# Attention scores with 128-row operands: queries' high and low parts stacked, keys doubled across the rows

## What is computed

```python
def rms_norm(x, g): return x * rsqrt(mean(x * x) + 1e-6) * g     # per head of 64
u = h @ w_qkv                                   # 16 query heads, 4 key heads, 4 value heads
q, k, v = split(u); q = rms_norm(q, qn_g); k = rms_norm(k, kn_g)
s = einsum('bnqkgd,bnskd->bkgnqs', q, k) / 8    # a chunk of 64 frames sees itself and the two before
s = s - slope[head] * |qpos - kpos|;  s = where(valid, s, -1e30)
p = exp(s - m) / (sum(exp(s - m)) + exp(sink - m));  o = p @ v;  x = x + o @ w_o
x = x + (silu(h @ w_gate) * (h @ w_up)) @ w_down                # h = rms_norm of x, d_ff 2816
```

## Time and profile before

| | |
|---|---|
| median of 3 runs | 2325.01 us (2325.01 to 2325.84) |
| the profiled execution's own time | 2324.02 us |
| its span in the trace | 2322.2 us |
| mean granted TensorE clock | 0.989 of full |
| busy: TensorE, VectorE, ScalarE, GpSimd | 2263.4, 1096.5, 1024.8, 1114.9 us |
| half A's attention (scores to values) | about 842 to 1224 us |
| half B's attention | about 1444 to 1824 us |

### The profile page before, as it was taken

How to read it: one execution, slowest core, us unless ns; L and a number is a source line. 1 busy time by engine, 2 the same in 40 slices (tenths; PEclk the granted TensorE clock), 3 DMA queues, 4 the chain that set the end, 5 groups by cost and what they waited for, 6 DMA issues and landing times.

```text
span 2322.2 us, 34761 instructions
## 1 busy us (share of the span) xinstructions
PE 2263.4 (97%) x14082; PEld 2034.6 (88%) x14082; DVE 1096.5 (47%) x1802; ACT 1024.8 (44%) x1639; POOL 1114.9 (48%) x573
## 2 busy tenths in 40 slices
PE   8998899999999999999999999999999999999999
PEld 7897678887888799999999898888888889999999
DVE  4986768863434434444443543444544242232223
ACT  6544655533425545445442465454554332222222
POOL 3787669975455433323333643333333444434442
PEclk9999899999999999999999999999999999999999
DMA  4111223332333322222222333222222223332322
GB/s 147 47 55 55 64 65 103 97 95 89 93 100 87 81 75 76 70 73 64 75 72 84 91 77 84 81 80 75 73 82 73 84 81 96 96 103 89 91 82 94
DMA packets 311437, 191.55 MB, mean 82 GB/s; under 512 B 40214, under 2 KB 285550, under 8 KB 311278
## 3 DMA queue, kind: packets, MB, share of 16 engines
q1 hardware_dynamic: 309400, 188.21, 27.2%
q10 hardware_dynamic: 1878, 1.11, 0.2%
HBM read 184.39 MB, written 5.10 MB: 82 GB/s over the span
## 4 chain that ended last, share of the span: by engine, by line
PE 91%; POOL 3%; DVE 2%; ACT 2%; issue 1%; DMA 0%; ACTq 0%; DVEq 0%; POOLq 0%
PE ps L337 41%; PE ps L346 21%; PE ps L553 14%; PE ps L560 7%; PE ps L523 2%; POOL accp L1920 2%; PE ps L483 1%; PE ps L509 1%; PE ps L355 1%; PE ps L484 1%; PE ps L485 1%; POOL wlo L1889 1%; PE ps L372 1%; DVE x L1573 1%; DVE sq L1382 1%
## 5 line engine op out<-in xcount | busy, mean ns | idle before, releaser
L1889 POOL TENSOR_TENSOR wlo<-raw,whi 128x1024 fp32r<-128x1024 f32 x342 | 839.7, 2455 | 1131.6 <-PE ps L346 802.9
L840 ACT ACTIVATE whi<-raw 128x1024 fp32r<-128x1024 f32 x342 | 361.6, 1057 | 638.7 <-PE ps L337 379.7
L337 PE MATMUL ps<-hBh,whi 128*128 128x272 f32 x2112 | 440.2, 289 | 8.2 <-DVE x L1573 3.3
L337 PE MATMUL ps<-hBl,whi 128*128 128x272 f32 x2112 | 439.4, 289 | 0.0
L337 PE MATMUL ps<-hAh,whi 128*128 128x512 f32 x1056 | 417.9, 396 | 18.5 <-DVE hAl L1387 10.9
L337 PE MATMUL ps<-hAl,whi 128*128 128x512 f32 x1056 | 415.4, 393 | 0.0
L1573 DVE TENSOR_TENSOR x<-ps,x 128x512 f32<-128x512 f32 (+1 forms) x368 | 258.3, 705 | 243.9 <-PE ps L560 181.4
L337 PEld LDWEIGHTS ps<-hBh,whi 128*128 128x128 f32 x2112 | 332.9, 189 | 11.4 <-issue 5.0
L337 PEld LDWEIGHTS ps<-hBl,whi 128*128 128x128 f32 x2112 | 331.6, 189 | 0.0
L346 PE MATMUL ps<-hBh,wlo 128*128 128x272 f32 x2112 | 293.7, 291 | 0.0
L346 PEld LDWEIGHTS ps<-hBh,wlo 128*128 128x128 f32 x2112 | 273.0, 188 | 6.3 <-issue 1.9
(11 more groups left out here) (249 smaller groups left out, 3196.3 us busy)
## 6 DMA issues: line engine op xcount, KB each, us to landing
raw<-in_w_gate_dram SPq DMA_DIRECT2D x88, 512.0 KB, 3.8
raw<-in_w_up_dram SPq DMA_DIRECT2D x88, 512.0 KB, 3.8
raw<-in_w_down_dram SPq DMA_DIRECT2D x88, 512.0 KB, 3.5
raw<-in_w_pw_dram SPq DMA_DIRECT2D x38, 512.0 KB, 3.9
raw<-in_w_qkv_dram SPq DMA_DIRECT2D x32, 256.0 KB, 3.7
raw<-in_w_o_dram SPq DMA_DIRECT2D x64, 128.0 KB, 2.9
stage<-in_x_prompt_dram SPq DMA_DIRECT2D x8, 512.0 KB, 5.4
raw<-in_w_qkv_dram SPq DMA_DIRECT2D x8, 512.0 KB, 3.9
```

What stands on the lines that cost most here:

```text
L337: ins = nc.tensor.matmul(o, whi[n % 2][:, P * k:P * (k + 1)], src[:, k, c0:c0 + w], start=(k == 0 and src is hi_[h]), stop=False)
L840: nc.scalar.activation(whi[n % 2][:], raw[n % 2][:], ACT.Copy).then_inc(w_hi, 1)
L1889: nc.gpsimd.tensor_tensor(wlo[n % 2][:], raw[n % 2][:], f(whi[n % 2][:]), ALU.subtract).then_inc(w_lo, 1)
```

## The change

The parts of a query head are stacked on all 128 partitions. For an even key group `hi_[h]` holds the head's high part on partitions 0-63 and its low part on 64-127; for an odd group `lo_[h]` holds the low part below and the high part above. `kkh` and `kkl` get one plane for each of the four key groups, with the same keys on both halves of the partitions. One matmul of 128 rows then gives high by `kkh` plus low by `kkh`, a second one the same with `kkl`: two matmuls a head for three. (The product low by low comes in with the second.)

- `q_high` and `q_low` become two instructions each, on 64 partitions and 512 columns; the samples' parts keep their own `qsh` and `qsl`, and the samples' scores stay as they were, with keys in `skh` and `skl`.
- `key_high` and `key_low` write each group's half of the partitions in two instructions. SP copies each half to the other half by four DMAs inside SBUF of 256 KB, issued ahead of the load of query tile 4's weights and behind a wait for `kv_lo`. In half A two more DMAs, ahead of query tile 6's, copy the last block of 128 keys to the front, where half B's first tile looks for it. Half B's keys overwrite half A's.
- TensorE waits for `k_twice` ahead of a half's first scores.
- The order of units goes from g0, g0, g1, g1, ... to g0, g1, g0, g1, g2, ..., because two groups now share a tile of `hi_` and `lo_` until both have been scored.
- Small arrays share space (`ssink` and `small` lie in `col`, `ckv` where `dwc` and `stc` were, the four `sco` are one array).

```diff
@@ -174,14 +180,12 @@
...
         with ExitStack() as c:
-            kkh = sb("kkh", [P, 2, TP + WIN + TS], F32R, c)
-            kkl = sb("kkl", [P, 2, TP + WIN + TS], F32R, c)
+            kkh = sb("kkh", [P, 4, 5 * P], F32R, c)
+            kkl = sb("kkl", [P, 4, 5 * P], F32R, c)
+            skh = sb("skh", [P, 2, WIN + TS], F32R, c)
+            skl = sb("skl", [P, 2, WIN + TS], F32R, c)
             vth = sb("vth", [P, 7, 2 * P], F32R, c)
             vtl = sb("vtl", [P, 7, 2 * P], F32R, c)
-            with ExitStack() as c2:
-                ckv = sb("ckv", [P, 2, 2 * P], F32, c2)
-            qsh = sb("qsh", [P, 2, 4 * TS], F32R, c)
-            qsl = sb("qsl", [P, 2, 4 * TS], F32R, c)
         with ExitStack() as c:
...
@@ -261,15 +266,19 @@
...
             u = 4 * beta + b + (32 if h == "B" else 0)
-            g, ip = beta // 2, beta % 2
+            g, ip = 2 * (beta // 4) + beta % 2, beta // 2 % 2
             t = b + (4 if h == "B" else 0)
...
             if t == 0:
-                return u, g, ip, b, 0, P, [(P, slot(0))]
-            return u, g, ip, b, P * (t - 1), 2 * P, [(P, slot(t - 1)), (P, slot(t))]
+                return u, g, ip, b, P, P, [(P, slot(0))]
+            return u, g, ip, b, P * b, 2 * P, [(P, slot(t - 1)), (P, slot(t))]
...
@@ -469,27 +478,25 @@
...
                     pe.wait_ge(kv_lo, 2 if h == "A" else 5)
+                    pe.wait_ge(k_twice, 16 * (4 if h == "A" else 10))
                     for key in [("vt", h, 0), ("vt", h, 1)] + ([("ck",), ("vs",)] if h == "B" else []):
...
                 if beta < 8:
-                    r = slice(HD * (g % 2), HD * (g % 2 + 1))
                     for s in range(2):
...
                         o = ps[:, 4, nk * s:nk * (s + 1)]
-                        qh, ql = (z[h][r, i, P * tl:P * (tl + 1)] for z in (hi_, lo_))
-                        kh, kl = (z[r, g // 2, k0:k0 + nk] for z in (kkh, kkl))
-                        nc.tensor.matmul(o, qh, kh, start=True, stop=False)
-                        nc.tensor.matmul(o, qh, kl, start=False, stop=False)
-                        ins = nc.tensor.matmul(o, ql, kh, start=False, stop=True)
+                        q = (hi_, lo_)[g % 2][h][:, i, P * tl:P * (tl + 1)]
+                        nc.tensor.matmul(o, q, kkh[:, g, k0:k0 + nk], start=True, stop=False)
+                        ins = nc.tensor.matmul(o, q, kkl[:, g, k0:k0 + nk], start=False, stop=True)
                 else:
...
                         qh, ql = qsh[r, b, :], qsl[r, b, :]
-                        kh, kl = (z[r, b, TP:TP + nk] for z in (kkh, kkl))
+                        kh, kl = (z[r, b, :] for z in (skh, skl))
                         nc.tensor.matmul(o, qh, kh, start=True, stop=False)
...
@@ -794,12 +801,22 @@
...
-            def qkv():
+            def qkv(h):
                 for gp in range(2):
...
                 for i in range(KD):
+                    if i == 4:
+                        sp.wait_ge(kv_lo, 2 if h == "A" else 5)
+                        for z in (kkh, kkl):
+                            for e in range(2):
+                                sp.dma_start(f(z[HD * (1 - e):HD * (2 - e), e:4:2, P:5 * P]),
+                                             f(z[HD * e:HD * (e + 1), e:4:2, P:5 * P])).then_inc(k_twice, 16)
+                    if i == 6 and h == "A":
+                        sp.wait_ge(k_twice, 16 * 4)
+                        for z in (kkh, kkl):
+                            sp.dma_start(f(z[:, :, 0:P]), f(z[:, :, 4 * P:5 * P])).then_inc(k_twice, 16)
                     n = slot(("q", i))
...
@@ -1103,7 +1120,8 @@
...
                     nc.scalar.activation(qsh[:, i // 4, TS * (i % 4):TS * (i % 4 + 1)], qraw[i][:, 512:512 + TS], ACT.Copy)
-                nc.scalar.activation(hi_[h][:, i, :], qraw[i][:, dest(h)], ACT.Copy).then_inc(h_hi[h], 1)
+                nc.scalar.activation(hi_[h][0:HD, i, 0:512], qraw[i][0:HD, 0:512], ACT.Copy)
+                nc.scalar.activation(lo_[h][HD:P, i, 0:512], qraw[i][HD:P, 0:512], ACT.Copy).then_inc(h_hi[h], 1)
...
@@ -1135,11 +1153,12 @@
...
                 src = qraw[7 - gp]
-                if h == "A":
-                    nc.scalar.activation(kkh[:, gp, 0:512], src[:, 0:512], ACT.Copy).then_inc(kv_hi, 1)
-                else:
-                    nc.scalar.activation(kkh[:, gp, 512:TP], src[:, 0:512], ACT.Copy)
-                    nc.scalar.activation(kkh[:, gp, TP + WIN:], src[:, 512:512 + TS], ACT.Copy).then_inc(kv_hi, 1)
+                if h == "B":
+                    nc.scalar.activation(skh[:, gp, WIN:], src[:, 512:512 + TS], ACT.Copy)
+                for e in range(2):
+                    r = slice(HD * e, HD * (e + 1))
+                    ins = nc.scalar.activation(kkh[r, 2 * gp + e, P:5 * P], src[r, 0:512], ACT.Copy)
+                ins.then_inc(kv_hi, 1)
...
@@ -1681,19 +1700,20 @@
...
                     nc.vector.tensor_tensor(qsl[z], qraw[i][:, 512:512 + TS], f(qsh[z]), ALU.subtract)
-                nc.vector.tensor_tensor(lo_[h][:, i, :], qraw[i][:, dest(h)], f(hi_[h][:, i, :]), ALU.subtract
+                e, o, n = slice(0, HD), slice(HD, P), slice(0, 512)
+                nc.vector.tensor_tensor(hi_[h][o, i, n], qraw[i][e, n], f(hi_[h][e, i, n]), ALU.subtract)
+                nc.vector.tensor_tensor(lo_[h][e, i, n], qraw[i][o, n], f(lo_[h][o, i, n]), ALU.subtract
                                         ).then_inc(h_ready[h], 1)
...
                 src = qraw[7 - gp]
-                if h == "A":
-                    nc.vector.tensor_tensor(kkl[:, gp, 0:512], src[:, 0:512], f(kkh[:, gp, 0:512]), ALU.subtract
-                                            ).then_inc(kv_lo, 1)
-                else:
-                    nc.vector.tensor_tensor(kkl[:, gp, 512:TP], src[:, 0:512], f(kkh[:, gp, 512:TP]), ALU.subtract)
-                    nc.vector.tensor_tensor(kkl[:, gp, TP + WIN:], src[:, 512:512 + TS], f(kkh[:, gp, TP + WIN:]),
-                                            ALU.subtract).then_inc(kv_lo, 1)
+                if h == "B":
+                    nc.vector.tensor_tensor(skl[:, gp, WIN:], src[:, 512:512 + TS], f(skh[:, gp, WIN:]), ALU.subtract)
+                for e in range(2):
+                    z = (slice(HD * e, HD * (e + 1)), 2 * gp + e, slice(P, 5 * P))
+                    ins = nc.vector.tensor_tensor(kkl[z], src[z[0], 0:512], f(kkh[z]), ALU.subtract)
+                ins.then_inc(kv_lo, 1)
...
```

More of the change, by code:

```diff
@@ L127, in build @@
         ones_h = sb("ones_h", [P, P])
-        col = sb("col", [P, NCOL])
-        dwc = sb("dwc", [P, TAPS * KD])
-        stc = sb("stc", [P, PAD * KD])
+        col = sb("col", [P, NCOL + 41])
+        with ExitStack() as c:
+            dwc = sb("dwc", [P, TAPS * KD], F32, c)
+            stc = sb("stc", [P, PAD * KD], F32, c)
+        with ExitStack() as c:
+            ckv = sb("ckv", [P, 2, 2 * P], F32, c)
+        qsh = sb("qsh", [P, 2, 4 * TS], F32R)
+        qsl = sb("qsl", [P, 2, 4 * TS], F32R)
         nsink = sb("nsink", [P, NH])
-        ssink = sb("ssink", [P, 4])
-        small = sb("small", [P, 37])
+        ssink = col[:, NCOL:NCOL + 4]
+        small = col[:, NCOL + 4:]
         eps, gqn, mn, den = small[:, 0:2], small[:, 2:3], small[:, 3:11], small[:, 11:19]
@@ L166, in build @@
             vo = sb("vo", [P, 2, 2 * P], F32, c)
-        sco = [sb(f"sco{s}", [P, 2, 2 * P + 1]) for s in range(4)]
+        sco = sb("sco", [P, 4, 2, 2 * P + 1])
+        sco = [sco[:, s] for s in range(4)]
         pth = sb("pth", [P, 4 * P], F32R)
@@ L216, in build @@
         hsq, hrs, qn_ready, kv_hi, kv_lo = sem("hsq"), sem("hrs"), sem("qn_ready"), sem("kv_hi"), sem("kv_lo")
+        k_twice = sem("k_twice")
         ko_ready, vo_ready = sem("ko_ready"), sem("vo_ready")
@@ L812, in _ @@
                 load(("p2", d), W2[:, :, P * d:P * (d + 1)])
-            qkv()
+            qkv("A")
             ffn(0, "B")
             wo()
-            qkv()
+            qkv("B")
             ffn(1, "A")
@@ L1168, in qkv_slot @@
                         full(act, ("ck",))
-                        nc.scalar.activation(kkh[:, :, TP:TP + WIN],
+                        nc.scalar.activation(skh[:, :, 0:WIN],
                                              ps[:, place["ck",][0], 0:256].rearrange("p (g n) -> p g n", g=2),
@@ L1720, in qkv @@
                             dve.wait_ge(kv_hi, 6)
-                            nc.vector.tensor_tensor(kkl[:, :, TP:TP + WIN],
+                            nc.vector.tensor_tensor(skl[:, :, 0:WIN],
                                                     ps[:, place["ck",][0], 0:256].rearrange("p (g n) -> p g n", g=2),
-                                                    f(kkh[:, :, TP:TP + WIN]), ALU.subtract).then_inc(fr(("ck",)), 1)
+                                                    f(skh[:, :, 0:WIN]), ALU.subtract).then_inc(fr(("ck",)), 1)
                             dve.wait_ge(kv_hi, 7)
```

## The result

| | before | after |
|---|---|---|
| median of 4 runs each | 2325.32 us (2325.01 to 2325.84) | 2288.37 us (2286.99 to 2289.63) |
| profiled execution, its span | 2324.02, 2322.2 | 2286.99, 2285.2 |
| busy: VectorE, ScalarE, GpSimd | 1096.5, 1024.8, 1114.9 | 1111.8, 1037.8, 1113.6 |

The change makes the kernel faster: the ratio of times is 0.9843, with an interval of 0.9831 to 0.9855. Forecast were 2284.8 us and a range of 2279 to 2298.

The account below looks back on a forecast made before the run. TensorE was taken as the bound. Fewer matmuls (15.0 us) and removed row switches (25) sum to 40.2 us, all else nothing: 2324.0 - 40.2 = 2283.8, as a median 2284.8 us, range 2279.0 to 2298.0.

Parts of the forecast that it names:

- The bound: Whole kernel: TensorE bounds it, busy 97% of the span and 91% of the chain that ended last.
- The switch: Score groups: going to 64-row operands and back costs TensorE 0.39 us a group; removing it saves 25 us.
- The count: Attention scores: 128 fewer matmuls at 0.118 or 0.11 us each save 15.0 us.
- The split instructions: Query and key parts on ScalarE and VectorE: each split costs a second full instruction, hidden behind TensorE, so nothing.
- The stretch by GpSimd: VectorE's two-input instructions stretch beside GpSimd's weight remainder, 2.85 us for 0.7; the split puts more there, costing nothing.
- The queue: SP's copies inside SBUF ahead of query weight loads: taken as costing nothing, 1.1 us late at most.
- the 3.6 of the bound: SP queue: upper limit of 3.6 us per 256 KB copy one after the other, 14.4 us for four.
- Any score group: Rival: the 0.39 us belongs to every score group, not 64 rows; only the matmul saving remains, 2310.0; chance 0.05.
- only the entering half: Rival: the step on entering score groups stays, 64 x 0.19 = 12.2 us come back, 2297.0; chance 0.08.
- spacing doubled: Rival: 128-row score matmuls are spaced at 0.23 us, so about 10 us of saving remain, 2315; chance 0.01.
- the copies: Rival: copies hold up SP's weight loads; at 10 us a copy 53 us are lost, 2338; chance 0.03.
- The stalls at VectorE: Rival: TensorE's 1.3 us waits for VectorE in the steps down multiply, 20 us come back, 2304; chance 0.04.

Follow-up runs that it names:

- the alternating run: Changed kernel with each head's first matmul reading only 64 rows and the second all 128; 2335.84 us.
- after_act_only: Changed kernel with 64 bytes saved ahead of the activation buffers: these at their old address, turned probabilities still 32 bytes off a multiple of 64; 2289.19 us.
- the runs with 64 and 32 bytes: Kernel before, with buffers from the activations on moved by 64 bytes: 2328.18 us; or from the turned probabilities on 32 bytes lower: 2327.47 us.
- the eight runs together: The changed kernel's first four runs and four more of it, unedited (median 2289.90 us); median of all 2289.3 us.
- the run on rows: Changed kernel with both matmuls per head reading only the 64 rows of the high part, all else kept; 2311.71 us.
- the third matmul: Changed kernel with a third matmul of 128 rows per head, the keys' low part taken twice; 2305.31 us.
- the run in series: Changed kernel with SP waiting for each of its ten copies inside SBUF to land before going on; 2289.61 us.

## Why the prediction was right

**The bound.** Right: TensorE's path carried the change, and the cut appeared on it.

**The switch, 25 us of the sum.** Right in cause and size. The 64 rows alone are worth 22.4 us by the medians (the runs of the one kernel spread over 2 us, those of the other over 3) and 24.9 by the traces; the alternating run has twice that. Over all groups of the two traces, scores and remainder together, a group gave 0.66 us in half B (0.64 forecast), and in half A 0.63 with 256 columns and 0.56 with 128 (0.63 and 0.56 forecast): 40.5 us for 40.2. Half B's 0.02 more come from the remainder, which fell to 1.82 on average and not to 1.86. That remainder behind transposes alone is no fixed floor, and scores between are not what removes it: `after_act_only`, with the same matmuls as the changed kernel, reads in half B's attention:

```profile
1676.35 1.86 PE ps L355 x8
```

What decides between 1.81 and 1.86 stays open.

**The count, 15.0 us.** Right: 15.5 in the kernel before, 16.0 in the changed one; by the traces of the two attentions 14.8 and 15.9.

**The split instructions at nothing.** Right in effect, the term mis-sized. ScalarE, the second part of a query and the weights' conversion behind it, and VectorE, in half B's second slot of the changed kernel, answering to the earlier trace rows:

```profile
1408.46 0.63 ACT L1124 ACTIVATE hBl<-qraw 64x512 fp32r<-64x512 f32 x1
1409.12 1.06 ACT L857 ACTIVATE whi<-raw 128x1024 fp32r<-128x1024 f32 x1
...
1410.23 0.69 DVE L1705 TENSOR_TENSOR hBl<-qraw,hBl 64x512 fp32r<-64x512 f32 x1
1410.95 0.69 DVE L1599 TENSOR_TENSOR s<-ps,s 128x512 f32<-128x512 f32 x1
...
1416.87 2.78 DVE L1604 TENSOR_TENSOR act0l<-s,act0h 128x512 fp32r<-128x512 f32 x1
```

A part takes its 0.62 and the next begins 0.62 to 0.66 later, not 0.55, and VectorE's lie 0.70 apart, not 0.6. So the busy times rose by 13.0 and 15.3 us where 11 and 12 were written. The conversion began with no idle time ahead of it, 0.7 us late where 0.4 was worked out: the conversions ahead of it lie 19.65 us earlier than in the kernel before, this one only 18.9. VectorE's gate product began right behind a low part and 0.4 us late by the same measure, where the prediction had left 0.5 us of room. So the slack is used up on both engines; TensorE had no wait from it (its waits from 1402 to 1440 us are none). The stretch by GpSimd went to the activations' low part (2.78) and not to the pairs; it cost nothing either.

**The queue at nothing.** Right. The copies landed in 4.8 and 5.8 us, above the 3.6 of the bound, with four out together; one at a time they took 4.5 and 3.0. In series the four held the queue from 765.1 to 778.7, 13.6 us, near the 14.4 of the bound.

**What failed.** The step "durations of everything untouched stay", which the sum used without saying it: it took 40.2 us off the profiled execution and left all else as it was. That execution became 37.0 us shorter, 3.2 less than forecast. By stage:

- Half B's attention missed 1.7. There 16 wide matmuls took 3.67 and not 3.63, the down steps 0.93 and 0.46 and not 0.92 and 0.45, the values 0.70 and not 0.69. Over the chain this is some 1.3 for the wide projection matmuls, 1.3 for the down matmuls and 0.3 for the values, 2.9 together; the groups gave 0.5 more than forecast. That overshoots the 1.7 by 0.7, as the pieces are rounded to 0.01.
- Half A's attention missed 0.5.
- The stages outside cost 2.3, of which 0.9 are the down matmuls of half A's first feed-forward net.
- The clock gave 1.3 back between the attentions: 0.5 + 1.7 + 2.3 - 1.3 = 3.2.

The prediction named the moved small arrays in the change and gave them no cost; the runs with 64 and 32 bytes show 2 to 3 us for either. The median is 3.6 above the forecast and not 3.2, since the profiled execution was the fastest of the four; the eight runs together have 2289.3, 4.5 above. In small part the closeness is luck: without the clock's dip, which only the trace of the kernel before has, the cut between the two traces would have been 35.5.

**The rivals.** "Any score group" and "only the entering half" are ruled out by the chain and by the run on rows, "spacing doubled" by the third matmul, the copies by the run in series. The stalls at VectorE stayed at three in half A's attention.

## What to carry to other kernels

A short group of matmuls on part of the rows, set between full-size ones, pays here for the way in and the way back, with four matmuls as with six; in a chain of pieces this is a first piece of 0.31 among 0.12s and a longer piece behind the group. Filling the rows with something useful (here the low part) saves it together with a matmul; if that isn't possible, put such matmuls together and never in alternation. When a change moves buffers, compare the spacing of matmuls it does not touch before looking for a cause in what it added.

## What the runs showed of the hardware

- A change between matmuls of 64 and of 128 rows costs 0.19 us each way: 0.31 against 0.12 for the next matmul of 256 columns, and 24.9 us for 128 changes and 48.3 for 256 between the same conversions. Matmuls of 64 and of 128 rows are otherwise spaced alike (0.12), and 64 stationary columns cost no such step (0.115 to 0.12).
- A shift of buffers by 64 or by 32 bytes a partition made matmuls, some of whose own operands had not moved, slower by up to 1% (3.63 to 3.67 us for 16), and the kernel by 0.1%. The cause is open.
- A copy of 256 KB inside SBUF landed in 4.8 to 5.8 us (medians of the two parts) with four under way, and in 3.0 to 4.5 us with the queue waiting for each.
- An instruction on 64 partitions and 512 columns took 0.62 us on ScalarE and 0.69 on VectorE, against 0.65 and 0.71 for 128 partitions and 544 columns: splitting one over the partitions costs almost a full second one.
